# Router logits from raw residual rows, the normalisation put on their 36 columns, and tile 1's normalised rows by ScalarE and GpSimd

## What is computed

```
h = layer_norm(ALPHA * h + merged @ w_out, ln1_g, ln1_b)        # over the 1024 features
group_logits  = h @ router_group_w  + router_group_b            # 4 columns
expert_logits = h @ router_expert_w + router_expert_b           # 4 groups x 8 columns
g = argmax(group_logits); the two best experts of group g, weights by softmax
y = sum over the two of weight * ((silu(h @ gate) * (h @ up)) @ down)
h = layer_norm(ALPHA * h + y, ln2_g, ln2_b)
```

## Time and profile before

| what | value |
|---|---|
| device time, median of 3 runs | 924.83 us (923.57 to 929.89) |
| span of the profiled execution, first to last instruction | 922.9 us; its own device time stands in no view |
| PE busy | 880.9 us, 95% of the span |
| DVE busy | 363.8 us, 39% |
| ACT busy | 176.9 us, 19% |
| POOL busy | 90.7 us, 10% |
| DMA | 218.65 MB read, mean 239 GB/s over the span |
| chain that ended last, by engine | PE 81%, DVE 7%, DMA 5%, SPq 3% |

### The profile page before, as it was taken

One profiled execution on the slowest core, in us unless ns is written; L12 is line 12 of the kernel. 1 busy time (PEld: TensorE's weight loads), 2 busy tenths in 40 slices (PEclk: granted clock), 3 DMA queues, 4 the chain that ended last, 5 costly groups with the idle time before them and its releaser, 6 DMA issues.

```text
span 922.9 us, 11935 instructions
## 1 busy us (share of the span) xinstructions
PE 880.9 (95%) x4893; PEld 545.6 (59%) x4893; DVE 363.8 (39%) x834; ACT 176.9 (19%) x363; POOL 90.7 (10%) x90
## 2 busy tenths in 40 slices
PE   6999799999999999899999999999998999999994
PEld 3446665766676774588868888668555333333331
DVE  5736825632233337565095321572255111101114
ACT  3125603100000000322323221341021111101001
POOL 0036300501101110300000000000020000000000
PEclk9999899999999999999999999999999999999998
DMA  9998765733334447023342222202797999999993
GB/s 367 425 415 311 290 258 205 297 114 134 134 165 183 183 182 273 0 92 136 138 178 97 93 92 92 92 9 92 320 396 257 373 398 423 422 419 424 417 418 149
DMA packets 24653, 218.29 MB, mean 237 GB/s; under 512 B 3658, under 2 KB 3938, under 8 KB 10003
## 3 DMA queue, kind: packets, MB, share of 16 engines
q1 hardware_dynamic: 21330, 205.76, 56.1%
q0 software_dynamic: 3264, 11.72, 3.5%
HBM read 218.65 MB, written 2.10 MB: 239 GB/s over the span
## 4 chain that ended last, share of the span: by engine, by line
PE 81%; DVE 7%; DMA 5%; SPq 3%; ACT 2%; issue 2%; DVEq 0%; POOLq 0%; ACTq 0%
PE psum L2381 12%; PE psum L2403 9%; PE psum L512 8%; PE psum L467 6%; PE psum L2169 6%; PE psum L1407 6%; DMA scr<-in_gates 3%; PE psum L2362 3%; PE psum L2141 3%; PE psum L771 3%; PE psum L1462 3%; PE psum L1431 3%; PE psum L591 2%; PE psum L2113 1%; SPq L2023 1%
## 5 line engine op out<-in xcount | busy, mean ns | idle before, releaser
L2381 PE MATMUL psum<-hT,ring 128*128 128x256 f32 x512 | 115.4, 379 | 1.1 <-issue 1.1
L2381 PEld LDWEIGHTS psum<-hT,ring 128*128 128x128 f32 x512 | 97.1, 190 | 26.7 <-issue 14.2
L512 PE MATMUL psum<-hT,ring 128*128 128x272 f32 x320 | 74.2, 393 | 0.0
L512 PEld LDWEIGHTS psum<-hT,ring 128*128 128x128 f32 x320 | 60.6, 190 | 12.9 <-issue 0.5
L2403 PE MATMUL psum<-scr 128*128 128x512 f32 x128 | 59.5, 592 | 0.0
L2842 DVE TENSOR_TENSOR scr<-ring 128x512 f32<-128x512 f32 x16 | 11.1, 691 | 121.6 <-PE psum L2403 121.6
L467 PE MATMUL psum<-hT,ring 128*128 128x256 f32 x256 | 58.1, 383 | 0.0
L2169 PE MATMUL psum<-ring,hT 128*128 128x512 f32 (+1 forms) x128 | 55.5, 598 | 2.3 <-ACT hT L2474 2.3
L1407 PE MATMUL psum<-ring,hT 128*32 128x512 f32 (+1 forms) x240 | 56.7, 594 | 0.1
L1407 PE MATMUL psum<-scr,hT 128*64 128x512 f32 (+1 forms) x192 | 51.6, 612 | 1.9 <-issue 1.9
L467 PEld LDWEIGHTS psum<-hT,ring 128*128 128x128 f32 x256 | 47.7, 190 | 6.8 <-issue 0.2
(11 more groups left out here) (561 smaller groups left out, 1261.5 us busy)
## 6 DMA issues: line engine op xcount, KB each, us to landing
ring<-in_stream SPq DMA_DIRECT2D x54, 2048.0 KB, 9.3
ring<-in_gates SPq DMA_DIRECT2D x9, 2048.0 KB, 22.0
ring<-in_downs SPq DMA_DIRECT2D x14, 1024.0 KB, 21.5
scr<-in_gates SPq DMA_DIRECT2D x6, 2048.0 KB, 26.4
scr<-in_gates SPq DMA_DIRECT2D x8, 1024.0 KB, 25.0
scr<-in_downs SPq DMA_DIRECT2D x8, 1024.0 KB, 16.0
scr<-in_stream SPq DMA_DIRECT2D x3, 2048.0 KB, 18.5
rowB<-in_rows POOLq DMA_DIRECT2D x5, 1024.0 KB, 11.9
```

The costliest lines, as they stand in the source:

```text
L512: last = mm(psum[:, g % 4, 0:L2], w[:, k, m * P:(m + 1) * P], hT[:, k, :], start=(k == 0), stop=(k == KD - 1))
L2381: last = mm(psum[:, f if f < 4 else 0, 0:NT], w[:, k, m * P:(m + 1) * P], hT[:, k, META:L2], start=(k == 0), stop=(k == KD - 1))
```

## The change

The router no longer reads normalised rows. With w the weights of a column, `sum(((x - mean) / dev * g + b) * w)` equals `(sum(x * g * w) - mean * sum(g * w)) / dev + sum(b * w)`. So the raw rows are turned and multiplied by `g * w`, and mean and deviation are put on 36 columns afterwards.

- POOL builds `g * w` and `b * w` (`rw_gain`) and sums them over the eight blocks of 128 features (`rw_sum`) once the router weights have landed; PE adds them over the partitions with one matmul by ones, put inside `out_proj` behind tile 0's transposes.
- PE turns raw rows (`turn_raw`): tile 0 at the old place, tile 1 in three pieces between router k-steps. Four `keep_warm` between the two tiles' routers are gone; three remain behind them.
- ACT evicts the turned rows by five plain copies in place of twelve activations, and makes tile 1's normalised rows (1024 columns) from a bias and a scale per row that DVE computes.
- DVE loses tile 1's `normalise`, `to_hT` and both operations on 1024 columns; it gains two small operations on the weight sums, six on the logits and one on the bias for ACT. Tile 0's `normalise` now stands behind the (1,0) residual.
- POOL gets gain and bias of tile 1: two operations of 1024 columns (L1278, L1279).
- SP's first ranked load also waits for `S.afv`, which POOL now raises. Several semaphores of the first block are merged into counts on the same engine (`att_a`, `att_v`), in the engine's own order.

```diff
 dve_second
-            for t in range(T):
-                residual(t, None, proj_wait("w_out2", 10))
-                normalise(5, t)
-            to_hT(4, V("g3"), V("b3"))
-            dve.wait_ge(S.in_row0, 48)
-            link(v.tensor_tensor(X[:, 1, :], X[:, 1, :], rowB[:, 0, 0, :], ALU.mult))
-            v.tensor_tensor(X[:, 1, :], X[:, 1, :], rowB[:, 0, 1, :], ALU.add).then_inc(S.afv, 1)
+            def router_logits(t):
+                dve.wait_ge(S.lg_mm, t + 2)
+                dve.wait_ge(S.ln_v, ln_count(5, t))
+                link(v.scalar_tensor_tensor(centred, rt_rows[:, 0:36], mv[:, t, 0:1], psum[:, 5 - t, 0:36],
+                                            ALU.mult, ALU.add))
+                v.scalar_tensor_tensor(every[:, NG * t:NG * t + NG, :].rearrange("p g e -> p (g e)"), centred[:, NG:36],
+                                       rstd[:, t:t + 1], rt_rows[:, 36 + NG:72], ALU.mult, ALU.add)
+                return v.scalar_tensor_tensor(lg[:, t, :], centred[:, 0:NG], rstd[:, t:t + 1], rt_rows[:, 36:36 + NG],
+                                              ALU.mult, ALU.add)
...
+            link(raw_half(1, 1))
+            raw_moments(1)
+            link(router_logits(0))
+            dve.wait_ge(S.ln_s, ln_count(5, 1))
+            link(v.reciprocal(rstd[:, 1:2], sd[:, 1:2]))
+            v.scalar_tensor_tensor(sd[:, 0:1], mv[:, 1, 0:1], -1.0, rstd[:, 1:2], ALU.mult, ALU.mult).then_inc(S.raw_x, 1)
+            link(router_logits(1))
 act_second
+            raw_out(5, 1, 6, KD, 0)
+            ln_sqrt(5, 1)
+            act.wait_ge(S.raw_x, 5)
+            sc.activation(X[:, 1, :], X[:, 1, :], ACT.Identity, bias=sd[:, 0:1], scale=rstd[:, 1:2]).then_inc(S.xn, 1)
 pool_tail
             link(nc.gpsimd.memset(xr[0], 0.0))
+            pool.wait_ge(S.xn, xn_count(5, 1))
+            link(nc.gpsimd.tensor_tensor(X[:, 1, :], X[:, 1, :], rowB[:, 0, 0, :], ALU.mult))
+            nc.gpsimd.tensor_tensor(X[:, 1, :], X[:, 1, :], rowB[:, 0, 1, :], ALU.add).then_inc(S.afv, 1)
             pool.wait_ge(S.afv, 1)
             pool.dma_start(hrows[P:NT], X[:, 1, :]).then_inc(S.hrow, 16)
 pe_experts
+            turn_raw(1, 0, 4, 2)
+            pe.wait_ge(S.raw_ev, 2)
+            router(0, 0, 4)
+            turn_raw(1, 4, 6, 3)
+            turn_raw(1, 6, KD, 0)
+            router(0, 4, KD).then_inc(S.lg_mm, 1)
...
+            router(1, 6, KD).then_inc(S.lg_mm, 1)
             keep_warm(6, 3)
```

More of the change, by code:

```diff
@@ L924, in act_second, with raw_out, dve_second @@
             weights(1)
-            for t in range(T):
[L926 to L931, removed]
+            def raw_out(n, t, k0, k1, bank):
+                act.wait_ge(S.xn_tr, 6 + n)
+                sc.copy(hT[:, k0:k1, tok(t)], psum[:, bank, 0:(k1 - k0) * P].rearrange("p (k n) -> p k n", n=P))\
+                    .then_inc(S.raw_ev, 1)
+            ln_sqrt(5, 0)
+            raw_out(1, 0, 0, 4, 0)
+            raw_out(2, 0, 4, KD, 1)
+            raw_out(3, 1, 0, 4, 2)
+            raw_out(4, 1, 4, 6, 3)
+            raw_out(5, 1, 6, KD, 0)
+            ln_sqrt(5, 1)
+            act.wait_ge(S.raw_x, 5)
+            sc.activation(X[:, 1, :], X[:, 1, :], ACT.Identity, bias=sd[:, 0:1], scale=rstd[:, 1:2]).then_inc(S.xn, 1)
             act_experts(act, link, ln_sqrt)
-        def dve_second(dve, v, link, chain, residual, normalise, to_hT, proj_wait):
+        def dve_second(dve, v, link, chain, residual, half_residual, normalise, proj_wait):
             for a in (ba, dN, kdN):
@@ L1490, in pe_dense @@
         def pe_dense(pe, mm):
+            pe.wait_ge(S.affine, 4)
+            pe.wait_ge(S.afv, 1)
+            for t in range(T):
+                for k in range(KD):
+                    last = nc.tensor.transpose(psum[:, 2 * t + k // 4, (k % 4) * P:(k % 4 + 1) * P],
+                                               X[:, t, k * P:(k + 1) * P], C("ident"))
+            last.then_inc(S.xg, 1)
+            pe.wait_ge(S.xgv, 1)
             pe.wait_ge(S.cmb, 4)
@@ L1591, in act_dense @@
         def act_dense(act):
+            act.wait_ge(S.xg, 1)
+            for t in range(T):
+                for half in range(2):
+                    last = nc.scalar.copy(hT[:, 4 * half:4 * half + 4, tok(t)],
+                                          b_(2 * t + half).rearrange("p (k n) -> p k n", n=P))
+            last.then_inc(S.xgv, 1)
             act.wait_ge(S.hrow, 32)
@@ L2003, in _ @@
                     sp.wait_ge(S.affine, 4)
+                    sp.wait_ge(S.afv, 1)
                 if n < FIXED_END:
@@ L2128, in transposes, with turn_raw, out_proj @@
                     last.then_inc(S.xn_tr, 1)
-            def out_proj(name, src, norm, pairs):
+            def turn_raw(t, k0, k1, bank):
+                pe.wait_ge(S.raw_x, 2 * t + k0 // 4 + 1)
+                for k in range(k0, k1):
+                    last = nc.tensor.transpose(psum[:, bank, (k - k0) * P:(k - k0 + 1) * P], X[:, t, k * P:(k + 1) * P],
+                                               C("ident"))
+                last.then_inc(S.xn_tr, 1)
+            def out_proj(name, src, pairs):
                 for half in range(2):
@@ L2903, in _ @@
             to_hT(3, V("ge"), V("be"))
-            dve_second(dve, v, link, chain, residual, normalise, to_hT, proj_wait)
+            dve_second(dve, v, link, chain, residual, half_residual, normalise, proj_wait)
 def lay_out(i):
```

155 lines of the change are left out of this document (92 added, 63 removed).

## The result

The changed kernel took 931.14 us (median of 20 runs, 926.33 to 934.46), the kernel before 926.12 us (median of 20, 923.05 to 930.34). The ratio on record is 1.0034, with a 95% interval from 1.0019 to 1.0050: 0.34% slower, 3.1 us of 924.83, and within the 1% that counts as no change. It is not the ratio of the two medians: they lie 5.0 us apart, and the means (930.7 and 926.7) 4.0. The times of either kernel fall into two groups, as experiments 1 and 2 show, and a median moves with the share of each. The forecast was 926.1 us, +1.3, from 920.3 to 929.8. By the ratio the changed kernel stands at 928.0 on the time that the forecast started from, so the sign, the class and the range came out, and the change cost some 2 us more than the sum gave; the median of 931.14 lies 1.3 us above the range.

The account below looks back on a forecast made before the run. It took the routing chain from `out_proj` to `perm`, which holds up the ranked expert loads, as the bound. Span 922.9 plus 0.15 (choice) and 1.1 (clock) gave 924.2, with 1.9 around it 926.1 us; range 920.3 to 929.8.

Parts of the forecast that it names:

- The logits: Router logits on DVE: the second pair of the choice of experts starts at 683.87 instead of 688.01, 4.1 us earlier.
- The hold: Choice of experts: DVE operations with two SBUF inputs wait for POOL's whole instructions, giving back 4.3 us, net +0.15.
- The first rival: Choice of experts: POOL and DVE do not hold each other; -4.1 or -3.2, 920.7 to 921.6 us; chance 0.14.
- The clock at the count: PE's count of experts: after 6.4 us of idling it runs at half clock, 2.45 us for 1.53, +0.9.
- The ranking: PE's ranking behind two `keep_warm` at half clock: some 0.8 us of lateness hides, so 0 to +0.3.
- The forecast's own range: Main case, hold plus half clock over the count: 924.8 to 927.8 us, chance 0.62.
- the third rival: Behind the ranking: half clock covers the gather and first `gate_up`, adding 6.6, 932.7 us; chance 0.06.
- The base: Whole kernel: profiled span 922.9 us, with 1.9 around it taken from the runs' median of 924.83.
- what runs differ by: Whole kernel: 0.7 us allowed in the forecast's own range for differences between runs.
- At nothing: POOL's weight operations, tile 0's moved `normalise`, the new waits and merged semaphores: expected to cost nothing.

Follow-up runs that it names:

- experiments 1 and 2: Both kernels run again unchanged: 1, the kernel before, 928.38 us; 2, the changed kernel, 930.33 us.
- Experiment 4: Changed kernel with POOL's two gain and bias operations for tile 1 on 32 of 1024 columns, the rest left out: 925.17 us.
- Experiment 3: Changed kernel with nine dummy matmuls in place of three behind the router's last one: 927.23 us.
- experiments 2 and 6: 2: changed kernel again, unchanged, 930.33 us; 6: changed kernel plus one dummy matmul ahead of each of two 0.77 us branch-stage waits, 927.02 us.
- experiment 5: Kernel before plus one dummy matmul ahead of each of PE's two 0.77 us waits for DVE in the branch stage: 924.86 us.
- experiments 9 and 12: 9: changed kernel, nine dummies behind the router, two in the branch stage, 925.54 us; 12: kernel before with the two branch dummies, 924.83 us.
- experiment 8: Changed kernel with tile 1's gain and bias moved from POOL to DVE behind the choice, five dummies behind the router, three behind the count: 926.23 us.

## Why the prediction was right or wrong, by its own steps

**The logits (4.1 us earlier)**: right. The choice starts 5.07 us behind the projection for 9.29, 4.2.

**The hold (4.3 given back, +0.15)**: right in mechanism and nearly in size. The two operations of 2.03 and 2.25 end with L1278 and L1279, the count starts 0.27 sooner rather than 0.15 later. Experiment 4 shows it by taking it away: 0.17 each, count 3.9 sooner. The Trainium skill's page "SBUF — State Buffer", section "SBUF: two separate sides", whose rule of a lock for the whole instruction spoke against this change, agrees with both runs: 2.03 and 2.25 beside POOL's 2.33 and 2.34, 0.17 beside 0.25 and 0.29. The first rival (no hold) fell.

**The clock at the count (+0.9)**: right in mechanism, a little short: 1.53 to 2.65, +1.1. Experiment 3 shows that it is the clock. That 2.10 us of idling were enough for a fall (experiment 4) is what the row of 1.90 us had suggested.

**The ranking (0 to +0.3)**: this term was mis-sized. From the count's reading to `perm` pass 4.67 us for 3.84, +0.83. The two dummies at half clock took 3.75 us, where I had put 3.0, from the ratio of 4.52 to 2.83; but those 4.52 were only mostly at half clock (0.60), so the ratio of 1.6 was too low. At a ratio of 2 the dummies end 1.8 to 1.9 us later, 1.0 to 1.1 with the 0.8 that hides taken off. The clock costs 1.96 us in all (experiment 3), not 1.1, and the sum for `perm` is +1.7, not +1.25. The forecast's own range is also added up wrongly at its lower end: its terms give 925.1, not 924.8.

**What came behind it**: the third rival, that the half clock lasts into the gather, had 0.06. It occurred in part, in two of the three profiles that have the changed stage unaltered (experiments 2 and 6), at about 1.8 us each rather than 6.6: the low clock covered most of the gather but ended before the first `gate_up`, which starts 2.5 us later still, and less than that arrives at the end. Two rows of idling, at 3.0 and 5.0 us behind the start of work, were too few to read a duration from. It was 6.1 us in the profile, where it ended just ahead of the gather, and 11.7 and 12.0 in those two; all three are over the 5 us that were to decide for this rival. For a fall into the gather 0.06 was too low.

**The base**: the largest miss is not of the change. The sum was made on an execution whose branch stage ran at full clock and on a median of 924.8, as 34 of 104 runs have it; the others stand 4.7 us higher. By their times, two of the three shown beside the profile were of the one kind and one, 929.89, of the other, and I spent 0.7 us on "what runs differ by". The 931.1 of the changed kernel is a median over both kinds, 12 of its 20 runs in the lower-clock group, where 9 of the 20 times of the kernel before lie above 927.6; with so even a mix the medians are partly chance, and so is the 5.0 between them. By the ratio the time, 928.0, lies just above the forecast's own range (927.8), and it is inside the whole one only because that took in part of the third rival: there luck had a hand. What the change itself costs is 1.4 us (experiments 5 and 6) to 3.3 us (within the groups of experiments 1 and 2), 3.1 by the ratio; the stage's +1.7, and the 1.8 behind it in some executions, make 1.7 to 3.5, and 0.6 less where the kernel before has its own fall at the ranking (experiment 5). The exact split between them is open, since one profile a run shows the stage and not every timed execution.

**At nothing**: the weights' folding, the waits for tile 1's rows and the merged semaphores show no cost clear of noise. The folding ended at 618.46, 60 us ahead of its first reader; with both falls of the clock filled and the hold still there, the changed kernel is even with the kernel before (experiments 9 and 12, +0.5 us of mean, from -0.6 to +1.6).

## What to carry to other kernels

Before moving work to an idle GpSimd, look at what VectorE runs at that moment: a chain of small operations with two SBUF inputs waits out each whole GpSimd instruction (2.03 and 2.25 us for 0.17), and the place to put the work is where VectorE itself waits (here the count, which hid 1.3 of 2.4 us at full clock). Whoever shortens TensorE's work ahead of a wait should ask what its clock does then, and cost everything in line behind it, dummies included, at the half clock (here the count took 1.7 times and the dummies 1.9 times as long). And a forecast should be made on the spread of the times shown as well as on one profile: where one of three runs stands 5 us off, look for the stage that has two lengths.

## What the runs showed of the hardware that I had not expected

TensorE's granted clock fell to 0.50 for 14 to 17 us in a stage where PE was busy all but two waits of 0.77 us; five profiles of changed kernels show it. By their mean clocks two thirds of the kernel before's runs have a fall of that size, for 4.7 us of time, and two dummy matmuls of 1.13 us put into those waits took it out of all 23 runs of that kernel. In the routing stage, too, the fall came in idling (of 6.00 us in the first profile, late in it), after 2.10 us of it in another, and within a row of dummies in a third (experiment 8, 685 to 688), and it lasted from 3 to 14 us. What decides its beginning and its length in a given execution is not settled by these runs. The Trainium skill's page "TensorE: Matmul & The Clock Gate", in its part on the HAM clock gate, says of a kernel's start that the monitor's window runs freely and that one kernel therefore meets it differently from run to run; the two groups of times fit that, but no run here shows the monitor itself.
